# Moving VectorE's eviction of the value product to the head of each softmax step

## What is computed

```python
for blk in range(seq // C_BLOCK):
    ...
    s = einsum('bhqd,bhkd->bhqk', qh[:, :, q0:q1], kh[:, :, :q1]) * scale
    s = s + c[:, :, q0:q1, None] - c[:, :, None, :q1]
    s = where(mask[None, None], s, -inf)
    p = softmax(s, axis=-1)
    outs.append(einsum('bhqk,bhkd->bhqd', p, vh[:, :, :q1]))
```

## Time and profile before

| | |
|---|---|
| median of 3 runs | 2771.62 us (2769.12 to 2774.09) |
| the profiled execution's own time | 2772.08 us |
| its span | 2770.2 us |
| TensorE busy | 2668.1 us (96%) |
| VectorE busy | 1453.9 us (52%) |
| ScalarE busy | 1121.3 us (40%) |
| mean granted TensorE clock | 0.975 |

### The profile page before, as it was taken

One profiled execution on the slowest core, in us unless ns is written; L12 is line 12 of the kernel. 1 busy time (PEld: TensorE's weight loads), 2 busy tenths in 40 slices (PEclk: granted clock), 3 DMA queues, 4 the chain that ended last, 5 costly groups with the idle time before them and its releaser, 6 DMA issues.

```text
span 2770.2 us, 33961 instructions
## 1 busy us (share of the span) xinstructions
PE 2668.1 (96%) x13218; PEld 2216.0 (80%) x13218; DVE 1453.9 (52%) x2735; ACT 1121.3 (40%) x1922; POOL 39.2 (1%) x62
## 2 busy tenths in 40 slices
PE   7999979999999999999999899999999999999997
PEld 6886668788888887778888787888888877788886
DVE  5744356664444647644444566644446486443444
ACT  4423244433463647432222344334636474322222
POOL 0000000000000100000000000000001000000000
PEclk9998699999999999999999999999999999999999
DMA  4310012213312432123232222123124221233322
GB/s 137 90 55 20 30 62 78 76 47 98 90 39 92 80 84 72 62 84 98 93 98 84 91 85 69 54 93 88 41 89 82 87 71 57 85 98 99 97 79 99
DMA packets 118430, 216.98 MB, mean 78 GB/s; under 512 B 14272, under 2 KB 21824, under 8 KB 118272
## 3 DMA queue, kind: packets, MB, share of 16 engines
q1 hardware_dynamic: 114528, 201.97, 23.4%
q0 software_dynamic: 3744, 12.85, 2.9%
HBM read 212.69 MB, written 2.10 MB: 78 GB/s over the span
## 4 chain that ended last, share of the span: by engine, by line
PE 37%; issue 19%; DVE 3%; ACT 1%; DMA 0%; POOL 0%; ACTq 0%; DVEq 0%; POOLq 0%
PE bank L533 17%; PE bank L536 13%; PE bank L635 2%; PE bank L624 1%; PE bank L600 1%; PE bank L567 1%; PE bank L601 1%; PE bank L664 1%; PE bank L681 1%; DVE wL L1334 0%; ACT wH L876 0%; DVE x L1828 0%; DVE gbuf L1928 0%; DVE sbufS L1903 0%; DVE sbufS L1905 0%
## 5 line engine op out<-in xcount | busy, mean ns | idle before, releaser
L1334 DVE TENSOR_TENSOR wL<-wraw,wH 128x1024 fp32r<-128x1024 f32 (+1 forms) x388 | 459.7, 1185 | 716.8 <-ACT wH L876 715.2
L876 ACT ACTIVATE wH<-wraw 128x1024 fp32r<-128x1024 f32 (+1 forms) x388 | 398.4, 1027 | 927.7 <-PE bank L533 499.3
L533 PE MATMUL bank<-wH,hH 128*128 128x512 f32 (+1 forms) x1248 | 503.9, 404 | 8.7 <-DVE wL L1334 3.7
L533 PE MATMUL bank<-wH,hL 128*128 128x512 f32 (+1 forms) x1248 | 482.2, 386 | 0.0
L533 PE MATMUL bank<-wL,hH 128*128 128x512 f32 (+1 forms) x1248 | 481.6, 386 | 0.0
L536 PE MATMUL bank<-hH,wH 128*128 128x512 f32 x1208 | 473.5, 392 | 2.8 <-ACT set L894 1.6
L536 PE MATMUL bank<-hH,wL 128*128 128x512 f32 x1208 | 470.4, 389 | 0.0
L536 PE MATMUL bank<-hL,wH 128*128 128x512 f32 x1208 | 470.2, 389 | 0.0
L533 PEld LDWEIGHTS bank<-wH,hH 128*128 128x128 f32 x1248 | 239.3, 192 | 62.5 <-issue 7.5
L533 PEld LDWEIGHTS bank<-wH,hL 128*128 128x128 f32 x1248 | 239.0, 192 | 48.4 <-issue 3.3
L533 PEld LDWEIGHTS bank<-wL,hH 128*128 128x128 f32 x1248 | 238.7, 191 | 48.0
(11 more groups left out here) (299 smaller groups left out, 2840.7 us busy)
## 6 DMA issues: line engine op xcount, KB each, us to landing
wraw<-in_w_in_dram SPq DMA_DIRECT2D x180, 512.0 KB, 3.5
wraw<-in_w_ffn_down_dram SPq DMA_DIRECT2D x44, 512.0 KB, 3.4
wraw<-in_w_ffn_gate_dram SPq DMA_DIRECT2D x40, 512.0 KB, 3.5
wraw<-in_w_ffn_up_dram SPq DMA_DIRECT2D x40, 512.0 KB, 3.5
wraw<-in_w_out_dram SPq DMA_DIRECT2D x24, 512.0 KB, 3.4
tab<-in_rpb_rev_dram POOLq DMA_DIRECT2D x32, 224.0 KB, 6.3
wraw<-in_w_up_a_dram SPq DMA_DIRECT2D x8, 512.0 KB, 3.4
wraw<-in_w_up_b_dram SPq DMA_DIRECT2D x8, 512.0 KB, 3.4
```

Of the source, the lines that this page charges most:

```text
L533: mm = pe.matmul(bank[t][:, 0:b.cols], act_part[:, k, t * P:(t + 1) * P], w_part[:, kk, :], start=first, stop=last)
L876: A(wH[:, u % W_SLOTS, 0:width], wraw[:, u % RAW_SLOTS, 0:width], ACT.Copy).then_inc(S["w_hi"], 1)
L1334: V.tensor_tensor(wL[:, u % W_SLOTS, 0:width], wraw[:, u % RAW_SLOTS, 0:width], wH[:, u % W_SLOTS, 0:width].bitcast(F32), ALU.subtract).th ...
```

## The change

In VectorE's copy of the softmax loop the block that evicts item s-4 is moved from behind the maximum of item s to the head of the step, in front of it. Its waits, operands and semaphores are the same, and so is everything on the other engines.

```diff
                 for s in range(max(len(items) + 4, len(side))):
+                    if 4 <= s < len(items) + 4 and weighs(items[s - 4]):
+                        it, y = items[s - 4], nth_y[s - 4]
+                        w, r = it["v"][1], rs[:, y % 4:y % 4 + 1]
+                        j = first_slot(it)
+                        total = lsum0[:, j:j + 1] if it["comp"] else lsum[:, y % 8:y % 8 + 1]
+                        src = bank[PV][:, 0:w]
+                        dve.wait_ge(S["pv_done"], y + 1)
+                        then(V.reciprocal(r, total))
+                        if kind == "fox":
+                            dst = merged[:, it["t"], SEQ + it["y"]:SEQ + it["y"] + w]
+                            V.scalar_tensor_tensor(out=dst, in0=src, scalar=r, in1=dst, op0=ALU.mult,
+                                                   op1=ALU.mult).then_inc(S["y_done"], 1)
+                        else:
+                            dst = ytok[:, it["t"], it["y"]:it["y"] + w]
+                            V.tensor_scalar(dst, src, r, None, ALU.mult).then_inc(S["y_done"], 1)
                     if s < len(items):
                         it, i, y = items[s], i0 + s, nth_y[s]
...
                             then(V.tensor_reduce(lowest, bank[SC + i % 2][:, 0:kmax], AX, ALU.max))
                             V.tensor_scalar(lowest, lowest, -SCALE, None, ALU.mult).then_inc(S["mx_done"], 1)
-                    if 4 <= s < len(items) + 4 and weighs(items[s - 4]):
...
-                            V.tensor_scalar(dst, src, r, None, ALU.mult).then_inc(S["y_done"], 1)
                     if 1 <= s <= len(items) and items[s - 1]["comp"] == 1:
```

## The result

The changed kernel takes 2743.92 us (2743.78 to 2744.12, 4 runs) against 2771.59 us (4 runs) for the kernel before: 27.7 us less, a ratio of 0.990 with a 95% interval of 0.9883 to 0.9917. The profiled execution's span is 2741.9 us, against 2770.2 us. The forecast was 2731 us, its range 2722 to 2763 us.

A forecast was written before the change was run, and what follows sets the result against it. TensorE, busy 96% of the span, bounds the kernel, with fox's half clock the larger loss. Upper bound 42.7 us (40 fox, 2.6 diff), less 2.7 kept back, gives 40 us off: 2731 us, range 2722 to 2763.

The forecast's parts named there:

- The waits: TensorE's waits for the eviction shrink: direct gain 8.9 us in fox, 2.6 us in diff.
- The clock: Fox's rounds: full clock holds once long waits go; 40 us upper bound including fox's direct gain, lower bound 0.
- The maximum now comes behind the eviction: VectorE's queue: late maximum comes 0.5 us later, hidden from TensorE; booked 0, without cover 2 us in fox.
- four narrow rounds: Fox from 263.22 to 337.61 us: 74.4 us fall to 44.1 at full clock, gain 30.3 us.
- kept back 2.7 us: Fox: allowance for one short clock fall behind the waits staying in steps 11, 13 and 15.
- signs of being wrong: Fox: rounds still at 0.50 with the waits gone, or a wait for the exponential at line 603 or 624.
- Rival 1: Fox near step 16: leftover waits still drop the clock, which stays low; 18 us gain, 2754 us; chance 0.22 with in-between cases.
- Rival 2: Fox: kind of matmul sets the clock, not waits; only 11.5 us direct gain, 2760 us; chance 0.16.
- Rivals 3 and 4: Fox's clock: 3, low level eats the gain, 2766 to 2777 us, 0.07; 4, earlier fall, 2779 us, 0.05.

The follow-up runs named there:

- filled kernel with the old order: Kernel before, with five added matmuls ahead of the transposes in each of fox's steps 7, 11, 13, 15, 19, 23, 27, 31: 2753.35 us, ratio 0.9937.
- run with step 27 put back: Changed kernel with the old order of eviction and maximum in fox's step 27 alone: 2749.74 us.
- run of the others alone: Kernel before with the eviction moved to the head in gqa, nat and diff only, fox in the old order: 2770.81 us, ratio 0.9999.
- ring cut: Changed kernel with ScalarE's extra work of fox put ahead of its exponential: 2733.00 us, ratio 0.9868.
- last waits filled: Changed kernel with ScalarE's extra work of fox first, plus added matmuls before the transposes of fox's steps 15, 18 and 23: 2730.18 us, ratio 0.9859.
- ScalarE's extras first: Kernel before, VectorE's old order, with ScalarE's extra work of fox ahead of its exponential: 2771.58 us, ratio 1.0005.

## Why the prediction was right, and by how much not

*The waits.* Right for step 7: its 1.23 us are gone. At line 635 they are gone in steps 19, 27 and 31 too, but TensorE then comes too early for ScalarE's copy at line 624: 0.32 us return in step 28 and 1.06 in step 32, nearly all that step 31 had given. The forecast had no such wait. Steps 11 and 13 kept 0.43 and 0.72 us, forecast 0.5 and 0.7. Step 14 got 0.66 us that I had not listed, step 15 kept 1.40 us against 0.55, step 23 0.48 us. Fox's total is 5.4 us instead of "3 or 4".

*The clock.* The main claim holds: most of the gain is not the waits but the level that they drop. Fox's waits for the eviction shrank by 6.8 us (12.2 to 5.4, with 1.4 us new at line 624), its seven rounds by 25.6. The filled kernel with the old order shows that the time can fall with step 7's wait filled and not saved. The run with step 27 put back is the clean case: the same TensorE instructions, one wait more, and the level falls. The first two rounds took 12.04 and 12.69 us, forecast 12.3 and 12.8; narrow rounds at full clock 10.31 to 13.20 us, forecast 11.0.

*The step that failed* is the one under "The maximum now comes behind the eviction": "What is queued behind it on VectorE (extras, split) is not later, since the sum of the work is the same. ... I book 0". The sum is the same only if VectorE never waits inside a step. In fox's steps 10 and 12 to 14 it waits for a square on ScalarE that stands behind the exponential of the very maximum that was pushed back, so each eviction put in front lengthens that ring by 0.40 us. Two such turns, 0.8 us, are about what step 15 waits beyond the forecast, 1.40 against 0.55 us. Step 15 has no side group; behind its wait the level falls, and stays down through the narrow rounds up to 282 us. With the ring cut the wait is 0.29 us and the fall is gone. In diff a chain of this kind takes 2.2 us back: the maximum behind the eviction, the exponential behind it (idle for 1.02 us until the maximum), ScalarE's row split, and VectorE's (idle for 1.44 us until that); it is read from one timeline, and no run cuts it.

*In terms of the sum:* the four narrow rounds took 57.0 us against 44.1 booked (four times the 11.0 us are 44.0), 12.9 us more, and the round of steps 12 to 15 2.0 us more. Of this the forecast had kept back 2.7 us. With the ring cut, the time is 2733 us and with the last waits filled 2730 us, so the forecast of 2731 us was the price of a clock that holds, and the change alone does not get there. One of its own signs of being wrong came half true: a round still shows 0.50, though with a wait in front of it that was not gone. That the time lies in the range owes something to luck: it takes the level's return at 282 us, for which no run gives a reason. In the kernel before, the low stretch that began at 265 us lasted to 306 us.

*The rivals.* Rival 1 had the right place, the fall near step 16, but put it down to waits of 0.7 and 0.55 us, where step 15 waited for 1.40; nor had it the length: the level came back at 282 us, and the time was 2744 instead of 2754 us. Rival 2 is refuted by the changed kernel against the one before, and by the run with step 27 put back. Rivals 3 and 4 did not occur.

The Trainium skill (TensorE: Matmul & The Clock Gate, section HAM oscillation — how this bites in real kernels) asks for idle gaps longer than any in this loop; the traces differ from it, with falls behind waits of 1.2 to 1.6 us. What the Trainium skill says on the same page, in the section A second HAM failure mode: psum-queue depth-cycling, that frequent short idles between groups of matmuls make the clock swing, the traces bear out.

*Open:* how long a wait must be. Over all twelve profiles, TensorE met 22 waits of 1.2 us or more before the value product at full clock, in steps 4 to 30; at or behind 20 of them the level fell, in the same step or the next. The two exceptions are step 11's, in the kernel before and in the run of the others alone, and the same wait was followed by a fall in the kernel before with ScalarE's extras first. Step 23's wait of 0.43 to 0.49 us was followed by a fall in three of six profiles, for 3, 7 and 41 us, and by none in the changed kernel's. Some versions scatter by up to 22 us between executions, while the changed kernel's four agree to 0.3 us. What decides in the single case, and what ends a low stretch, was not found.

## What to carry to other kernels

Where TensorE works through a stretch of small matmuls, a wait of one microsecond can cost several times its length through the clock: compare the granted clock round by round before pricing waits, and look first at the steps with no dense work in them. Before moving an instruction ahead of another in an in-order queue, follow the one pushed back through the other engines; if something later in the same queue waits for its result, the moved one is now part of that ring. And a second edit that does nothing alone may be worth much after the first.

## What was unexpected

Adding 40 matmuls made a kernel 18 us faster. The level, once low, stayed so from 254.7 to 282 us although TensorE was busy for 18.63 of 18.90 us in the first round of that stretch. In every version TensorE ran at 0.50 at the start of fox, and came to 1.00 within the loop's first three steps, not in the same one each time; in the twelve profiles that alone moves the time by up to 4.5 us.
